# Cross-attention scores and values of a transformer kernel: fp32 matmuls exchanged for three fp32r passes over split operands

## Chip, cores and metric

The kernel runs on one core of one Trainium2 chip. The metric is the device time of one launch in microseconds. TensorE (PE in the rows) does the matmuls, VectorE (DVE) and ScalarE (ACT) the work between them, SyncE (SP) issues most of the DMAs.

## What is computed

The program is two transformer blocks in a row on a 512 x 1024 input. The second block contains, twice (layers 0 and 1), a cross-attention from 512 positions into 256 memory tokens with 4 heads of 256 features:

```
q = rmsnorm_2((h @ w_q).reshape(B, S, X_HEADS, X_HEAD_DIM), q_gain)
kv = (mem_n @ w_kv).reshape(B, M, 2, X_HEADS, X_HEAD_DIM)
k = rmsnorm_2(kv[:, :, 0], k_gain)
v = kv[:, :, 1]
s = jnp.einsum('bqhd,bkhd->bhqk', q, k).astype(jnp.float32) * (X_HEAD_DIM ** -0.5)
p = jax.nn.softmax(s, axis=-1)
o = jnp.einsum('bhqk,bkhd->bqhd', p.astype(v.dtype), v)
return o.reshape(B, S, D_MODEL) @ w_o
```

Around it stand the feed-forward networks, a sliding-window attention with gated linear attention, a differential attention and a stick-breaking attention. They are not touched by the change.

## The kernel before

Every large product is made as three fp32r matmuls over operands split in two: a high part (the value rounded to fp32r) and a low part (the value less its high part). The product is then high*high + high*low + low*high. Lines 606 to 608 are the three passes of a weight slab, lines 1134 to 1138 and 1156 to 1158 those of the memory's keys and values. The weights come as slabs of 128 x 2048 through two landing buffers `w_raw`; ScalarE rounds each to `w_hi` (`high`, line 1351) and VectorE subtracts to `w_lo` (`low`, line 2049). Each of the two holds four slabs.

The products of the cross-attention itself are different: the scores (line 1196) and the values (line 1235) are plain fp32 matmuls of 128 x 256, which the trace records as two matmul records each.

Cross-attention, function `cross` on each engine, runs in two parts. First come projections: keys and values of head 0, then the queries of the four heads, with the norms on ScalarE and VectorE behind them. Then TensorE runs a loop over eight items (four heads, two halves of 256 positions each) plus two steps in which the pipeline empties. Step `i` of this loop is, on TensorE:

1. scores of item `i` (4 matmuls),
2. in steps 1, 3 and 4 the sums of squares of a key head (`sum_squares`, line 639),
3. a projection that lies beside the items: keys of heads 1, 2, 3 in steps 0, 2, 3, values of head 1 in step 1, and a half of the values of heads 2 and 3 in each of the steps 4 to 7; in step 8, four tiles of the output projection instead,
4. the four transposes (line 1220) of the probabilities of item `i-1`,
5. the values of item `i-2` (4 matmuls); in step 9 two tiles of the output projection go ahead of them.

VectorE works through its own loop in the order in which it is written, and the order is fixed by hand. Step `i` is: in steps 4, 6, 8 and 10 first the four instructions (`operand`, lines 1904 and 1906) that cut the outputs of one head for the output projection; then the row maxima of item `i` (lines 2725 and 2728), the scaling of item `i-1`'s probabilities (`probabilities`, lines 2182 to 2188), the norms of a query or key head (`norm_queries`, `norm_keys`, line 1916), the copy of the projected keys or values out of PSUM (`keep_keys` line 2652, `keep_values` line 2659), and `low` for a weight slab. In step 8 the probabilities of item 7 go ahead of the operands.

ScalarE makes the exponentials (line 1824), the inverse norms (lines 1387, 1389), `high`, the copy `copy_turned` of the transposed probabilities from PSUM to `cr_pt` (line 1539) and the squares of the keys.

Both layers run the same code. VectorE instructions are mostly followed by a wait for the engine's own semaphore (`done`), so that they do not overlap.

Of the kernel before, what the change touches and what calls it, by code (L numbers as in the profile page):

```python
# [15 lines left out]
P = 128  # L16
SEQ = 512
# [135 lines left out]
def build(nc, wstream, gains, conv_w, lam_in, base, rope, later, gla_masks, alibi, gate_up,  # L153
          x_in, p_in, mem_in, out):
    ctx = ExitStack()
    with ctx:
# [41 lines left out]
        with ExitStack() as s:  # L198
            cr_q = sb("cr_q", [P, KT, SEQ], FP32, s)
# [6 lines left out]
            cr_pt = sb("cr_pt", [P, 2, 4 * P], FP32, s)  # L206
# [22 lines left out]
        with ExitStack() as s:  # L229
            od_hi_even = sb("od_hi_even", [P, 2, FAR], FP32R, s)  # L230
        sums = sb("sums", [P, SEQ])
# [51 lines left out]
        with ExitStack() as s:  # L283
            cr_pad = sb("cr_pad", [P, 8], FP32, s)
            cr_mhi = sb("cr_mhi", [P, KT, MEM], FP32R, s)
            cr_mlo = sb("cr_mlo", [P, KT, MEM], FP32R, s)
            cr_v = sb("cr_v", [P, 2, D], FP32, s)
        with ExitStack() as s:
# [52 lines left out]
        pt_copied = sem("pt_copied")  # L341
        pv_ready = sem("pv_ready")
# [118 lines left out]
        def key_parts():  # L461

            return query_hi[:, 1, 0:MEM], query_lo[:, 1, 0:MEM]

# [116 lines left out]
        def _(pe):  # L581
# [533 lines left out]
            def cross(at, layer):  # L1115
# [70 lines left out]
                for i in range(N + 2):  # L1186
                    if i < N:
                        h, half = CROSS_ITEMS[i]
                        if half == 0:
                            pe.wait_ge(rs_used, job0 + (5 + h if h else 2))  # L1190
                        if i >= 2:
                            pe.wait_ge(e_ready, i0 + i - 1)
                        for j in range(2):
                            at_q = slice((2 * half + j) * P, (2 * half + j + 1) * P)
                            for k in range(2):
                                mm = mm_(ps[:, 4 + i % 2, j * MEM:(j + 1) * MEM], cr_q[:, 2 * h + k, at_q],
                                         cr_k[:, 2 * h + k, :], start=(k == 0), stop=(k == 1))
# [13 lines left out]
                    if 1 <= i <= N:  # L1211
# [3 lines left out]
                        if i >= 3:  # L1215
                            pe.wait_ge(pt_copied, i0 + i - 2)
# [6 lines left out]
                    if i >= 2:  # L1223
                        h, half = CROSS_ITEMS[i - 2]
                        pe.wait_ge(pt_copied, i0 + i - 1)
                        pe.wait_ge(acc_free, at + VALUE_SLABS[h] + 3)
# [6 lines left out]
                        for d in range(2):  # L1233
                            for a in range(2):
                                mm = mm_(ps[:, out_bank(h, d), half * 256:half * 256 + 256],  # L1235
                                         cr_v[:, a, (2 * h + d) * P:(2 * h + d + 1) * P],
                                         cr_pt[:, (i - 2) % 2, a * 256:a * 256 + 256], start=(a == 0), stop=(a == 1))
# [657 lines left out]
        def _(dve):  # L1895
# [752 lines left out]
            def cross(of, at, layer):  # L2648
# [30 lines left out]

                def first_keys():  # L2680
# [17 lines left out]
                for h in range(4):  # L2698
# [5 lines left out]
                    add_pair(h)  # L2704
                    low(at + QUERY_SLABS[h] + 4)
                i0, N = n["it"], len(CROSS_ITEMS)
                for i in range(N + 3):
                    it = i0 + i
                    if i >= 3 and CROSS_ITEMS[i - 3][1]:
                        h = CROSS_ITEMS[i - 3][0]  # L2710
                        if i == N:
                            probabilities(it - 1, cr_s, MEM, ring=2)
                        for d in range(2):
# [258 lines left out]
```

## Time and profile before

| what | value |
|---|---|
| time, median of 3 runs (lowest to highest) | 2560.86 us (2560.44 to 2560.95) |
| the profiled execution's own time | 2560.95 us |
| its span, from first to last instruction | 2559.1 us |
| TensorE busy | 2540.1 us, 99% of the span |
| VectorE busy | 1596.4 us, 62% |
| ScalarE busy | 911.6 us, 36% |
| granted TensorE clock over the span | 1.000 |
| the eight-item loop of layer 0 | 1278.58 to 1352.5 us |

A TensorE record lasts longer than the time by which it holds up the next one, since matmuls are pipelined; what a matmul costs is read from start to start.

### The profile page before, as it was taken

The page shows a single profiled execution, that of the slowest core. Times are in us where ns is not written, and L with a number is a line of the kernel's source. Part 1 is how long each engine was busy: PE and PEld are TensorE (multiplying, and loading weights), DVE is VectorE, ACT ScalarE, POOL GpSimd, SP SyncE. Part 2 cuts the span into 40 slices and gives each one's busy share as a digit, 9 for nine tenths or more (in the row PEclk, how much of TensorE's full clock was granted, in tenths as well). Part 3 has the DMA queues.
Part 4 walks back from the last instruction along what each step waited for, and adds up shares of the span by engine and source line. Part 5 has one row for each costly group of instructions (what it writes and reads, how often), then busy time and mean ns, then how long its engine had stood idle before and what let it go on. Part 6 is the DMA issues. An engine that isn't in the chain of part 4 may idle for free.

```text
span 2559.1 us, 31974 instructions
## 1 busy us (share of the span) xinstructions
PE 2540.1 (99%) x12548; PEld 2106.0 (82%) x12548; DVE 1596.4 (62%) x1976; ACT 911.6 (36%) x1184; POOL 10.2 (0%) x24
## 2 busy tenths in 40 slices
PE   9999999999999999999999999999999999999999
PEld 7888888778888888877898888888886888888887
DVE  6444468866444468677765747476357665775755
ACT  5222234543222245344443323233146343432322
POOL 0000001000000000000000000000000000000000
PEclk9999999999999999999999999999999999999999
DMA  5323233112322232212321222323210232232322
GB/s 184 101 83 100 96 110 121 67 50 99 103 87 98 99 115 101 99 50 99 132 97 63 104 101 83 114 83 124 94 66 13 87 116 83 84 116 83 100 97 82
DMA packets 37410, 241.91 MB, mean 95 GB/s; under 512 B 4416, under 2 KB 7280, under 8 KB 9136
## 3 DMA queue, kind: packets, MB, share of 16 engines
q1 hardware_dynamic: 34736, 233.78, 26.9%
q10 hardware_dynamic: 1920, 5.22, 0.6%
q0 software_dynamic: 640, 1.31, 0.2%
q8 instruction: 81, 1.33, 0.2%
q14 instruction: 33, 0.27, 0.0%
HBM read 236.89 MB, written 2.10 MB: 93 GB/s over the span
## 4 chain that ended last, share of the span: by engine, by line
PE 93%; DVE 5%; ACT 1%; issue 1%; DMA 0%; DVEq 0%; ACTq 0%
PE ps L606 24%; PE ps L607 24%; PE ps L608 24%; PE ps L1235 1%; PE ps L624 1%; PE ps L626 1%; PE ps L625 1%; PE ps L767 1%; PE ps L1268 1%; PE ps L1292 1%; PE ps L1283 1%; DVE w_lo L2049 1%; PE ps L769 1%; PE ps L768 1%; PE ps L1304 1%
## 5 line engine op out<-in xcount | busy, mean ns | idle before, releaser
L606 PE MATMUL ps<-op_hi,w_hi 128*128 128x512 f32 x2056 | 800.9, 390 | 0.2 <-DVE op_lo L1930 0.2
L607 PE MATMUL ps<-op_lo,w_hi 128*128 128x512 f32 x2056 | 800.5, 389 | 0.0
L608 PE MATMUL ps<-op_hi,w_lo 128*128 128x512 f32 x2056 | 800.4, 389 | 0.0
L1351 ACT ACTIVATE w_hi<-w_raw 128x2048 fp32r<-128x2048 f32 x217 | 414.2, 1910 | 485.9 <-PE ps L608 299.8
L2049 DVE TENSOR_TENSOR w_lo<-w_raw,w_hi 128x2048 fp32r<-128x2048 f32 x217 | 497.0, 2292 | 38.9 <-ACT w_hi L1351 22.5
L606 PEld LDWEIGHTS ps<-op_hi,w_hi 128*128 128x128 f32 x2056 | 386.4, 188 | 81.5 <-issue 1.4
L608 PEld LDWEIGHTS ps<-op_hi,w_lo 128*128 128x128 f32 x2056 | 386.3, 188 | 80.5
L607 PEld LDWEIGHTS ps<-op_lo,w_hi 128*128 128x128 f32 x2056 | 386.3, 188 | 80.0
L2014 DVE SCALAR_TENSOR_TENSOR x<-ps,x 128x512 f32<-128x512 f32 x134 | 92.6, 691 | 310.8 <-PE ps L608 293.1
L606 PE MATMUL ps<-h_hi,w_hi 128*128 128x512 f32 x692 | 269.5, 389 | 0.0
L608 PE MATMUL ps<-h_hi,w_lo 128*128 128x512 f32 x692 | 269.2, 389 | 0.0
L607 PE MATMUL ps<-h_lo,w_hi 128*128 128x512 f32 x692 | 269.2, 389 | 0.0
L2097 DVE TENSOR_TENSOR sil<-ps,rs_x 128x512 f32<-128x512 f32 x44 | 30.4, 691 | 211.8 <-PE ps L608 209.4
L1464 ACT ACTIVATE conv_buf<-u_buf,cw 128x512 f32<-128x512 f32 x88 | 63.2, 725 | 261.0 <-DVE u_buf L2080 261.0
L606 PEld LDWEIGHTS ps<-h_hi,w_hi 128*128 128x128 f32 x692 | 129.9, 188 | 27.5 <-DVE h_lo L2108 0.6
L608 PEld LDWEIGHTS ps<-h_hi,w_lo 128*128 128x128 f32 x692 | 129.9, 188 | 27.0
L607 PEld LDWEIGHTS ps<-h_lo,w_hi 128*128 128x128 f32 x692 | 129.9, 188 | 27.0
L1469 ACT ACTIVATE sil<-sil 128x512 f32<-128x512 f32 x44 | 27.8, 632 | 338.3 <-DVE sil L2097 338.3
L2080 DVE TENSOR_TENSOR u_buf<-ps,rs_x 128x512 f32<-128x512 f32 x44 | 30.4, 691 | 82.2 <-PE ps L608 82.2
L2089 DVE SCALAR_TENSOR_TENSOR conv_buf<-u_buf,cw,conv_buf 128x511 f32<-128x511 f32 x88 | 66.1, 751 | 20.5 <-ACT conv_buf L1464 11.0
L1396 ACT ACTIVATE sq<-x 128x512 f32<-128x512 f32 x80 | 48.2, 621 | 77.9 <-DVE sums L1942 74.2
L2092 DVE SCALAR_TENSOR_TENSOR conv_buf<-u_buf,cw,conv_buf 128x510 f32<-128x510 f32 x88 | 66.0, 750 | 10.5 <-DVE conv_buf L2089 1.4
(373 smaller groups left out, 3083.2 us busy)
## 6 DMA issues: line engine op xcount, KB each, us to landing
w_raw<-in_wstream_dram SPq DMA_DIRECT2D x217, 1024.0 KB, 4.8
cr_m<-in_mem_dram ACTq DMA_DIRECT2D x2, 1024.0 KB, 4.9
w_raw<-in_wstream_dram SPq DMA_DIRECT2D x7, 256.0 KB, 7.7
x<-in_x_dram SPq DMA_DIRECT2D x3, 512.0 KB, 7.5
out_dram<-x SPq DMA_DIRECT2D x3, 512.0 KB, 2.6
m_s<-m_q POOLq DMA_DIRECT2D x16, 64.0 KB, 2.5
ev_s<-in_alibi_dram ACTq DMA_DIRECT2D x1, 1024.0 KB, 5.0
m_c<-in_rope_dram ACTq DMA_DIRECT2D x1, 640.0 KB, 4.2
```

What stands on the lines that cost most here:

```text
L606: mm_(o, w_hi[:, c % 4, w], hi[:, k, 0:cols], start=(k == 0), stop=False)
L607: mm_(o, w_hi[:, c % 4, w], lo[:, k, 0:cols], start=False, stop=False)
L608: mm = mm_(o, w_lo[:, c % 4, w], hi[:, k, 0:cols], start=False, stop=(k == kt - 1))
L1351: f_(w_hi[:, c % 4, :], w_raw[:, c % 2, :], ACT.Copy).then_inc(w_hi_ready, 1)
L1396: f_(to[:, n["xsq"] % 2, 0:src.shape[1]], src, ACT.Square).then_inc(xsq_ready, 1)
L1464: f_(conv_buf[:, j, :], u_buf[:, j, :], ACT.Copy, scale=tap).then_inc(tap_ready, 1)
L2014: ins = v.scalar_tensor_tensor(x[:, 2 * d + j, :], acc(c, j), half, x[:, 2 * d + j, :], ALU.mult, ALU.add)
L2049: v.tensor_tensor(w_lo[:, c % 4, :], w_raw[:, c % 2, :], w_hi[:, c % 4, :].bitcast(FP32), ALU.subtract).then_inc(w_ready, 1)
L2080: v.tensor_tensor(u_buf[:, 0, :], acc(c, 0), rs_x[:], ALU.mult).then_inc(scaled_ready, 1)
L2089: v.scalar_tensor_tensor(buf[:, 1:SEQ], u[:, 0:SEQ - 1], w1, buf[:, 1:SEQ], ALU.mult, ALU.add).then_inc(v_step, 1)
L2092: v.scalar_tensor_tensor(buf[:, 2:SEQ], u[:, 0:SEQ - 2], w0, buf[:, 2:SEQ], ALU.mult, ALU.add).then_inc(v_step if j else conv_ready, 1)
L2097: v.tensor_tensor(sil[:, c % 2, :], acc(c, 0), rs_x[:], ALU.mult).then_inc(scaled_ready, 1)
```

## The change

The scores and values of the cross-attention become three fp32r passes each, like the projections. The operands have to be split for this, all of it on VectorE: `cut_queries`, `cut_keys` and `cut_values` are a rounding copy and a subtraction per head, and `cut_turned` is one subtraction per item. The high part of the turned probabilities is what ScalarE writes to `cr_pt` anyway, which now has the type fp32r. The values of an item are multiplied in two groups: eight matmuls with the high part of the probabilities, then a wait for `pt_cut`, then four with the low part. The low parts of queries, keys and values take the place of the originals in memory; the high parts lie in the operand buffers `op_hi` and `op_lo`, those of head 0's queries and keys in a new tile `cr_first`. Scores wait for `score_parts`, values for `value_parts`. Tile allocations and semaphores are left out here.

```diff
                         h, half = CROSS_ITEMS[i]
                         if half == 0:
-                            pe.wait_ge(rs_used, job0 + (5 + h if h else 2))
+                            pe.wait_ge(score_parts, 4 * layer + h + 1)
...
                             for k in range(2):
-                                mm = mm_(ps[:, 4 + i % 2, j * MEM:(j + 1) * MEM], cr_q[:, 2 * h + k, at_q],
-                                         cr_k[:, 2 * h + k, :], start=(k == 0), stop=(k == 1))
+                                o, q_hi, k_hi = ps[:, 4 + i % 2, j * MEM:(j + 1) * MEM], queries_hi(h), keys_hi(h)
+                                mm_(o, q_hi[:, k, at_q], k_hi[:, k, :], start=(k == 0), stop=False)
+                                mm_(o, q_hi[:, k, at_q], cr_klo[:, 2 * h + k, :], start=False, stop=False)
+                                mm = mm_(o, cr_qlo[:, 2 * h + k, at_q], k_hi[:, k, :], start=False, stop=(k == 1))
...
                         if i >= 3:
-                            pe.wait_ge(pt_copied, i0 + i - 2)
+                            pe.wait_ge(pt_cut, N * layer + i - 2)
...
-                        pe.wait_ge(acc_free, at + VALUE_SLABS[h] + 3)
+                        pe.wait_ge(value_parts, 4 * layer + h + 1)
...
                         for d in range(2):
                             for a in range(2):
-                                mm = mm_(ps[:, out_bank(h, d), half * 256:half * 256 + 256],
-                                         cr_v[:, a, (2 * h + d) * P:(2 * h + d + 1) * P],
-                                         cr_pt[:, (i - 2) % 2, a * 256:a * 256 + 256], start=(a == 0), stop=(a == 1))
+                                o, at_h = ps[:, out_bank(h, d), half * 256:half * 256 + 256], slice(d * P, (d + 1) * P)
+                                p_hi = cr_pt[:, (i - 2) % 2, a * 256:a * 256 + 256]
+                                mm_(o, values_hi(h)[:, a, at_h], p_hi, start=(a == 0), stop=False)
+                                mm_(o, cr_vlo[:, a, (2 * h + d) * P:(2 * h + d + 1) * P], p_hi, start=False, stop=False)
+                        pe.wait_ge(pt_cut, N * layer + i - 1)
+                        for d in range(2):
+                            for a in range(2):
+                                o, at_h = ps[:, out_bank(h, d), half * 256:half * 256 + 256], slice(d * P, (d + 1) * P)
+                                p_lo = cr_ptlo[:, (i - 2) % 2, a * 256:a * 256 + 256]
+                                mm = mm_(o, values_hi(h)[:, a, at_h], p_lo, start=False, stop=(a == 1))
...
+                def cut_queries(h):
+                    heads = slice(2 * h, 2 * h + 2)
+                    v.tensor_copy(queries_hi(h), cr_q[:, heads, :]).then_inc(v_step, 1)
+                    done(v_step)
+                    last = v_step if h else score_parts
+                    v.tensor_tensor(cr_qlo[:, heads, :], cr_q[:, heads, :], queries_hi(h).bitcast(FP32),
+                                    ALU.subtract).then_inc(last, 1)
+                    done(last)
...
+                def cut_turned(it):
+                    dve.wait_ge(pt_copied, it + 1)
+                    v.tensor_tensor(cr_ptlo[:, it % 2, :], ps[:, 6 + it % 2, :], cr_pt[:, it % 2, :].bitcast(FP32),
+                                    ALU.subtract).then_inc(pt_cut, 1)
+                    done(pt_cut)
...
                     add_pair(h)
+                    if h == 0:
+                        cut_keys(0)
+                    elif h == 1:
+                        cut_queries(0)
                     low(at + QUERY_SLABS[h] + 4)
...
                         if i == N:
                             probabilities(it - 1, cr_s, MEM, ring=2)
+                            cut_turned(it - 2)
...
                     if 1 <= i < N:
                         probabilities(it - 1, cr_s, MEM, ring=2)
+                    if 2 <= i < N or i == N + 1:
+                        cut_turned(it - 2)
                     if i == 1:
                         norm_queries(3)
                     if i < N:
                         if i in CROSS_SUMS:
                             norm_keys(CROSS_SUMS[i][0])
+                            cut_keys(CROSS_SUMS[i][0])
...
                     if i - 1 in CROSS_ENDS:
                         low(at + CROSS_ENDS[i - 1] + 4)
+                    if i in (0, 2, 3):
+                        cut_queries(max(i, 1))
+                    if i in (1, 2, 5, 7):
+                        cut_values(i // 2 if i > 2 else i - 1)
```

## Rows read from the trace of the kernel before

**Rows 1.** The page: busy time of the engines.

```profile
PE 2540.1 (99%) x12548; PEld 2106.0 (82%) x12548; DVE 1596.4 (62%) x1976; ACT 911.6 (36%) x1184; POOL 10.2 (0%) x24
```

**Rows 2.** Busy time by stretch: stretch, length, then each engine's busy time (instructions).

```profile
1278.58:1352.30 73.72, 72.66 (x482) 66.93 (x480) 50.18 (x79) 33.09 (x65) 0.00 (x0) 1.00 0.28 92
```

**Rows 3.** TensorE's timeline in steps 0 to 3 of layer 0: start, length, what.

```profile
1280.43 0.28 PE L1136 MATMUL ps<-cr_mlo,w_hi 128*128 128x256 f32 x1
...
1285.96 1.02 PE L683 MATMUL ps<-sq,sums_r 128*128 128x512 f32 x2
...
1288.92 1.10 PE L639 MATMUL ps<-sq,sums_r 128*128 128x256 f32 x4 [0.21 <-ACT sq L1363]
...
1289.98 0.28 PE L1157 MATMUL ps<-w_hi,cr_mlo 128*128 128x256 f32 x1
...
1295.32 0.60 PE L1220 MATMUL ps<-ident,cr_s 128*128 128x128 f32 x4
...
1303.37 1.89 PE L1235 MATMUL ps<-cr_pt,cr_v 128*128 128x256 f32 x8
1305.10 1.89 PE L1196 MATMUL ps<-cr_k,cr_q 128*128 128x256 f32 x8
```

**Rows 4.** VectorE's instructions over the whole span, grouped by line and form.

```profile
L2771 DVE TENSOR_TENSOR od_lo<-od_s,od_hi 128x1024 fp32r<-128x1024 f32 x8 | 9.8, 1225 | 0.3
...
L2769 DVE CAST od_hi<-od_s 128x1024 fp32r<-128x1024 f32 x8 | 5.5, 694 | 0.3
...
L1960 DVE TENSOR_TENSOR query_lo<-sq,query_hi 128x512 fp32r<-128x512 f32 x6 | 4.2, 693 | 0.2
...
L1958 DVE CAST even_hi<-sq 128x512 fp32r<-128x512 f32 x8 | 3.4, 428 | 0.3
```

**Rows 5.** VectorE's timeline in the loop of layer 0; the bracket is idle time before.

```profile
1288.82 0.69 DVE L2725 TENSOR_REDUCE stat<-ps 128x2 f32<-128x512 f32 x1 [1.89 <-PE ps L1196]
...
1289.75 0.17 DVE L2182 RECIPROCAL stat<-stat 128x2 f32<-128x2 f32 x1
...
1290.73 1.54 DVE L1916 SCALAR_TENSOR_TENSOR cr_q<-cr_q,g_sb,rs 128x512 f32<-128x512 f32 x2
...
1295.59 0.69 DVE L2659 TENSOR_TENSOR cr_v<-ps,rs_col 128x512 f32<-128x512 f32 x1 [2.29 <-PE ps L1158]
...
1298.53 0.68 DVE L2725 TENSOR_REDUCE stat<-ps 128x2 f32<-128x512 f32 x1
...
1307.03 0.69 DVE L2725 TENSOR_REDUCE stat<-ps 128x2 f32<-128x512 f32 x1 [0.81 <-PE ps L1196]
...
1309.89 1.01 DVE L1916 SCALAR_TENSOR_TENSOR cr_k<-cr_k,g_sb,rs 128x256 f32<-128x256 f32 x2 [1.00 <-ACT rs L1389]
...
1316.55 0.68 DVE L1904 CAST op_hi<-ps 128x512 fp32r<-128x512 f32 x1
...
1319.44 0.69 DVE L2725 TENSOR_REDUCE stat<-ps 128x2 f32<-128x512 f32 x1
```

**Rows 6.** VectorE's timeline, step 6 of the same loop.

```profile
1333.64 0.69 DVE L2725 TENSOR_REDUCE stat<-ps 128x2 f32<-128x512 f32 x1
...
1337.49 2.29 DVE L2049 TENSOR_TENSOR w_lo<-w_raw,w_hi 128x2048 fp32r<-128x2048 f32 x1 [1.98 <-ACT w_hi L1351]
```

**Rows 7.** TensorE's timeline, steps 4 and 9 of the same loop.

```profile
1321.37 0.66 PE L1220 MATMUL ps<-ident,cr_s 128*128 128x128 f32 x4 [0.37 <-DVE cr_s L2188]
...
1350.74 1.89 PE L1235 MATMUL ps<-cr_pt,cr_v 128*128 128x256 f32 x8
```

**Rows 8.** TensorE's timeline at the start of the kernel, same columns.

```profile
6.25 2.50 PE L841 MATMUL ps<-w_hi 128*128 128x256 f32 x10 [6.25 <-ACT w_hi L1571]
...
10.68 0.63 PE L608 MATMUL ps<-op_hi,w_lo 128*128 128x512 f32 x1
...
20.73 0.39 PE L606 MATMUL ps<-op_hi,w_hi 128*128 128x512 f32 x1
20.96 0.39 PE L607 MATMUL ps<-op_lo,w_hi 128*128 128x512 f32 x1
```

More of the change, by code:

```diff
@@ L198, in build @@
         with ExitStack() as s:
+            with ExitStack() as t:
+                cr_qlo = sb("cr_qlo", [P, KT, SEQ], FP32R, t)
             cr_q = sb("cr_q", [P, KT, SEQ], FP32, s)
@@ L205, in build @@
             cr_s = sb("cr_s", [P, 2, 2, MEM], FP32, s)
-            cr_pt = sb("cr_pt", [P, 2, 4 * P], FP32, s)
+            cr_pt = sb("cr_pt", [P, 2, 4 * P], FP32R, s)
+            with ExitStack() as t:
+                cr_klo = sb("cr_klo", [P, KT, MEM], FP32R, t)
             cr_k = sb("cr_k", [P, KT, MEM], FP32, s)
@@ L230, in build @@
             od_hi_even = sb("od_hi_even", [P, 2, FAR], FP32R, s)
+        with ExitStack() as s:
+            cr_ptlo = sb("cr_ptlo", [P, 2, 4 * P], FP32R, s)
         sums = sb("sums", [P, SEQ])
@@ L286, in build @@
             cr_mlo = sb("cr_mlo", [P, KT, MEM], FP32R, s)
+            with ExitStack() as t:
+                cr_vlo = sb("cr_vlo", [P, 2, D], FP32R, t)
             cr_v = sb("cr_v", [P, 2, D], FP32, s)
+            cr_first = sb("cr_first", [P, 3, SEQ], FP32R, s)
         with ExitStack() as s:
@@ L341, in build @@
         pt_copied = sem("pt_copied")
+        score_parts = sem("score_parts")
+        value_parts = sem("value_parts")
+        pt_cut = sem("pt_cut")
         pv_ready = sem("pv_ready")
@@ L463, in key_parts, with queries_hi, keys_hi, values_hi @@
             return query_hi[:, 1, 0:MEM], query_lo[:, 1, 0:MEM]
+        def queries_hi(h):
+            return op_hi[:, 2 * h:2 * h + 2, :] if h else cr_first[:, 0:2, :]
+        def keys_hi(h):
+            tile = op_lo[:, 2 * h, :] if h else cr_first[:, 2, :]
+            return tile.rearrange("p (k n) -> p k n", k=2)
+        def values_hi(h):
+            return op_lo[:, 2 * h + 1, :].rearrange("p (a n) -> p a n", a=2)
         def query_parts(h):
@@ L2678, in norm_queries, with cut_keys, cut_values @@
                     head_norm([cr_q[:, 2 * h + k, :] for k in range(2)], [gcol(f"xq{layer}", k) for k in range(2)])
+                def cut_queries(h):
[6 more added lines that the diff above has]
+                    done(last)
+                def cut_keys(h):
+                    heads = slice(2 * h, 2 * h + 2)
+                    v.tensor_copy(keys_hi(h), cr_k[:, heads, :]).then_inc(v_step, 1)
+                    done(v_step)
+                    last = score_parts if h else v_step
+                    v.tensor_tensor(cr_klo[:, heads, :], cr_k[:, heads, :], keys_hi(h).bitcast(FP32),
+                                    ALU.subtract).then_inc(last, 1)
+                    done(last)
+                def cut_values(h):
+                    head = slice(h * 256, (h + 1) * 256)
+                    v.tensor_copy(values_hi(h), cr_v[:, :, head]).then_inc(v_step, 1)
+                    done(v_step)
+                    v.tensor_tensor(cr_vlo[:, :, head], cr_v[:, :, head], values_hi(h).bitcast(FP32),
+                                    ALU.subtract).then_inc(value_parts, 1)
+                    done(value_parts)
+                def cut_turned(it):
[3 more added lines that the diff above has]
+                    done(pt_cut)
                 def first_keys():
```

## The prediction

> **What bounds the kernel.** I read the page first: TensorE is busy for 99% of the span, VectorE for 62% [rows 1]. That says only that, averaged over the kernel, time taken from TensorE is time gained. The change lies in two short loops, one a layer, so the second view is the busy time of that stretch: of 73.72 us TensorE is busy for 72.66 and VectorE for 50.18 [rows 2]. VectorE's 79 instructions each stand about 0.03 us apart, 2.4 us, so it has some 21.1 us free. The third view is TensorE's timeline there, for what a matmul costs from start to start; the fourth VectorE's timeline, since the change puts work into a queue in a fixed order, and the brackets show where that queue had slack. Layer 1 has the same waits, so I work out layer 0 and double it.
>
> **What TensorE saves.** The eight fp32 records of an item's values hold it from 1303.37 to 1305.10, 1.73 us; the scores have the same number and form of records [rows 3]. Each becomes twelve fp32r matmuls of 128 x 256, a form that the projections already have: from 1280.43 to 1285.96 there are 47 of them, 0.118 us each, from 1289.98 to 1295.32 again 47, 0.114 each [rows 3]. Twelve cost 1.36 to 1.41, so a group saves 0.32 to 0.37. There are 16 groups a layer: 5.1 to 5.9 us a layer, 10 to 12 us in all, if nothing else decides.
>
> **What VectorE gets.** All forms of the new instructions are in the trace: a rounding copy of 128x512 takes 0.43, of 128x1024 0.69; a subtraction 0.69 and 1.225 [rows 4]. With 0.03 behind each, a cut of a key or value head is 1.19 us, of a query head 1.98, a `cut_turned` 0.73 (one source is in PSUM; the operands' line 1906 has that form and the four of a head go by at 0.72 each, 1316.55 to 1319.44 [rows 5]). In the loop: three query heads 5.9, three key heads 3.6, four value heads 4.7, eight turned items 5.8, together 20.0 us. The cuts of keys 0 and queries 0 come earlier, while TensorE projects queries, where VectorE has waits of 1.5 and 3.7 us behind them; they cost nothing, and 0 to 0.4 us if that cover is thinner than I read. So VectorE needs 50.2 + 2.4 + 20.0 = 72.6 us for a loop that TensorE alone would now do in about 68. VectorE becomes the bound. Whether the loop gets longer than 73.7 depends on where its queue still has to wait, so I walk through it.
>
> **The walk, layer 0.** Units from [rows 5]: maxima and probabilities 1.91 (1288.82 to 1290.73), the probabilities alone 0.98 (from 1289.75); norms of queries 1.57, of keys 1.04; a `keep` with a `low` 2.94 (1295.59 to 1298.53), so `low` 2.21 and `keep` 0.73; operands of a head 2.89.
> Step 0: VectorE was free at 1286.93. `cut_queries(1)` fills this gap; maxima(1) start at 1288.92, 0.1 late. TensorE gains 0.7 by now and loses it: it waits at line 639 for ScalarE's squares until 1288.92 [rows 3], and ScalarE is not faster.
> Step 1: 1.91 + 1.57 + 1.04 + `cut_keys(1)` ends at 1294.6; the wait for the projected values until 1295.59 covers that. `low` ends at 1298.53 as before, then `cut_values(0)`: maxima(2) 1299.7.
> Step 2: +1.91 + 0.73 = 1302.35; the key projection ends at 1302.6, and with 0.27 of latency `keep_keys(2)` goes at 1302.85; `low` to 1305.8, `cut_queries(2)` and `cut_values(1)` to 1308.95. Maxima(3) were at 1307.03.
> Step 3: maxima, probabilities and `cut_turned(1)` to 1311.6; `norm_keys(2)` needs ScalarE's inverse norm, 2.86 after the maxima (1307.03 to 1309.89 before): 1311.8; then 1.04 + 1.19 + 0.73 + 2.21 + 1.98 (`cut_queries(3)`) = 1318.95.
> Step 4: operands to 1321.85, maxima and probabilities to 1323.75. TensorE, which had been up to 1.4 us ahead of before, is ready for the transposes of item 3 at about 1319.1: it stands idle for 4.7 us. They start at 1323.8; before, 1321.37 [rows 7]. `cut_turned(2)`, the wait for ScalarE again (1324.7), `norm_keys(3)`, `cut_keys(3)`, `low`: 1329.1.
> Step 5: 1.91 + 0.73 + 0.73 + `cut_values(2)` = 1333.7.
> Step 6: operands to 1336.55, +1.91 + 0.73 = 1339.2. `low` waits for ScalarE's `high`, 3.85 after the maxima (1333.64 to 1337.49 [rows 6]): 1340.4 to 1342.6. This is the only real gap left in VectorE's queue, 1.2 us.
> Step 7: 1.91 + 0.73 + 0.73 + 1.19 = 1347.2. Step 8: 0.98 + 0.73 + 2.89 + 2.21 = 1354.0. Step 9: `cut_turned(7)`, queued behind that `low` though TensorE needs it first, to 1354.7.
> TensorE: the transposes of item 6 go at 1344.6, and with output tiles, item 7's transposes and item 6's values it is through the eight high matmuls of item 7 at 1353.4. It waits for `pt_cut`, restarts 0.1 late, and four matmuls (0.46) end at 1355.25. Before they ended at 1350.74 + 1.73 = 1352.47 [rows 7]. Behind this everything is paced by TensorE as before (the last operands are ready 1.2 us before it wants them), so the loss stays: 2.8 us a layer, 5.6 in all.
> The other new waits cost nothing: `score_parts` for head 2 is set at 1314.05, just when TensorE arrives (up to 0.1, and covered by the idle time in step 4); `value_parts` and the other `pt_cut` are set earlier than wanted. `low` comes up to 4.5 us later for six slabs, and so do SyncE's loads into the freed buffer, but each slab's `high` follows more than 5 us behind its load, and DMA engines are 28% busy [rows 2]. ScalarE's copy into fp32r costs what its copy into fp32 did: bound 0 to 0.1 us an item, in its idle time.
>
> **A rule that speaks against it further.** The trace shows what idleness can do: behind the 6.25 us of idle time at the start ten 128x256 matmuls took 2.50 us, 0.23 apart, twice the 0.114 above, which is the 1.2 instead of the 2.4 GHz level, and a 512-column record still lasts 0.63 at 10.68 against 0.39 at 20.73 [rows 3, 8]. The granted clock is 1.00 in the whole of the loop [rows 2], where the longest idle stretch was 0.5 us; mine has one of 4.7. If the clock fell there for the 4.6 us that it was low at the start, the transposes of item 3 and the values and scores behind them would take 2.3 us more; part of that VectorE hides, and by the walk the scores of item 5 and the values of item 3 would each come about 0.5 late for VectorE, 0.6 us a layer together.
> The Trainium skill ("TensorE: Matmul & The Clock Gate", section "Why this matters for your kernels") has it that idle gaps between bursts of matmuls put the clock back to half; by it the time would be some 1.2 us longer. The trace agrees for the start, and shows no such gap later.
>
> **Rivals.** *VectorE keeps up* (faster, 0.07): the additions fit into the 21.1 us of free time, and TensorE paces the loop. For it: 20.0 is less than 21.1. Against: in the walk 3.1 us of it stay unused (1.0 in step 1, 0.5 in step 2, 0.2 and 0.2 for the inverse norms, 1.2 in step 6), and `cut_queries(2)`, `cut_values(1)` and `cut_queries(3)`, 5.15 us, all stand ahead of step 4's transposes. The point is the transposes of item 3: VectorE would have to be through probabilities(3) at 1319.1 instead of 1323.75. It would give 2560.95 - 11.8 + 1.4 (step 1's wait) = 2550.5 us.
> *The queue loses less* (within 0.2%, 0.36): my walk keeps three waits for ScalarE, 0.2 + 0.2 + 1.2 us. If they close, the loop is 1.1 us longer instead of 2.8: 2563.2 us. For it: ScalarE is busy for 33 of 73.7 us. Against: its work hangs on VectorE's maxima, at distances that the rows show. A walk that is 10% too long lies here too.
> *The clock falls as well* (0.15): 2560.95 + 5.6 + 1.2 = 2567.8 us.
> *Plain forecast* (0.42): 2560.95 + 5.6 = 2566.5 us.
>
> **The numbers.** The sum is made against the profiled execution, 2560.95 us, 0.09 above the median of the three runs. 0.2%, about what a measurement of this kernel can tell from no change, is 5.1 us, so a forecast of 5.6 lies close to the line. Slower by more: 0.57 (forecast and clock); within: 0.36; faster: 0.07. The likeliest case's own range is 2565.4 to 2568, from 2.3 to 3.5 us a layer: TensorE's pace of 0.114 or 0.118, restarts behind waits, cover thinner ahead of the loop. The range for 8 in 10 leaves out the fast rival and some of each tail: 2559.5 to 2571, its upper end by the clock case with the 10 new idle stretches of two layers each costing 0.3 us more at their restarts.
>
> **What the new profile would show.** Right: VectorE nearly without a gap from 1298 to 1354, about 70 us busy in the loop, one gap of over 1 us before the `low` of step 6; TensorE idle for 4 to 5 us before the transposes of item 3 and 1.3 to 1.5 us each before those of items 4 and 5 and before the low matmuls of item 7; twelve matmuls in 1.36 to 1.41 us; a loop of 76 to 77 us, twice. Wrong: a loop below 74 us, or no wait of TensorE for `cr_s` in step 4. What would make me wrong: VectorE's copies slower or faster on these layouts than in [rows 4], ScalarE earlier than its distances, or a clock below 1.00 behind step 4.

## The result, and the profile of the changed kernel

The changed kernel takes 2568.28 us (median of 8 runs, 2567.45 to 2570.03); the kernel before, run beside it, 2561.46 us (2560.44 to 2564.51). The ratio is 1.0025, 95% interval 1.0016 to 1.0035: slower by 6.8 us. The profiled execution took 2568.33 us, its span is 2566.5 us, and the granted clock over the span is 0.998.

The page's line of busy times: against [rows 1], TensorE is busy for 4.8 us less, and VectorE for 44.1 us more.

```profile
PE 2535.3 (99%) x12676; PEld 2107.6 (82%) x12676; DVE 1640.5 (64%) x2040; ACT 911.9 (36%) x1184; POOL 10.2 (0%) x24
```

The two loops, by stretch: length, busy time of TensorE, of its weight loads, of VectorE, ScalarE and GpSimd, granted clock, DMA share, GB/s.

```profile
1278.81:1355.86 77.05, 70.21 (x545) 67.69 (x544) 68.58 (x106) 33.12 (x65) 0.00 (x0) 0.98 0.26 85
2086.29:2164.05 77.76, 70.95 (x545) 68.44 (x544) 68.69 (x106) 33.13 (x65) 0.00 (x0) 0.96 0.26 85
```

The loop of layer 0 begins with the first scores at 1278.81 and ends where the output projection goes on, at 1355.86: 77.05 us, against 1278.58 to 1352.47, 73.9, before. Layer 1 takes 77.76. VectorE's busy time went from 50.2 to 68.6 us, and the clock is no longer 1.00 as in [rows 2].

TensorE's timeline, layer 0: start, length, line, what, and in brackets how long it had stood idle and for whom.

```profile
1278.81 0.28 PE L1222 MATMUL ps<-cr_first 128*128 128x256 f32 x1
1278.92 0.28 PE L1223 MATMUL ps<-cr_klo,cr_first 128*128 128x256 f32 x1
1279.04 0.28 PE L1224 MATMUL ps<-cr_first,cr_qlo 128*128 128x256 f32 x1
...
1289.16 0.67 PE L664 MATMUL ps<-sq,sums_r 128*128 128x256 f32 x2 [0.82 <-ACT sq L1397]
...
1304.95 0.28 PE L1222 MATMUL ps<-op_lo,op_hi 128*128 128x256 f32 x1
...
1306.39 0.60 PE L664 MATMUL ps<-sq,sums_r 128*128 128x256 f32 x2
...
1324.31 0.79 PE L1247 MATMUL ps<-ident,cr_s 128*128 128x128 f32 x4 [4.24 <-DVE cr_s L2222]
1324.75 0.56 PE L1264 MATMUL ps<-cr_pt,op_lo 128*128 128x256 f32 x1
1325.33 0.41 PE L1264 MATMUL ps<-cr_pt,op_lo 128*128 128x256 f32 x1
...
1355.28 0.74 PE L1271 MATMUL ps<-cr_ptlo,op_lo 128*128 128x256 f32 x4 [1.02 <-DVE cr_ptlo L2742]
1355.86 0.40 PE L1193 MATMUL ps<-op_hi,w_hi 128*128 128x512 f32 x1
```

What to see: twelve score matmuls take 1.44 us (1304.95 to 1306.39) where the eight records before took 1.73 [rows 3]. The transposes of item 3 (line 1247), which waited 0.37 us before [rows 7], wait 4.24. The last low pass waits 1.02 for the cut of the turned probabilities. The lead that TensorE gained in step 0 is gone in step 1, where it waits 0.82 for ScalarE's squares.

VectorE's timeline of the same loop, same columns, answers to [rows 5] and [rows 6].

```profile
1287.17 0.69 DVE L2716 CAST op_hi<-cr_q 128x1024 fp32r<-128x1024 f32 x1
1287.90 1.23 DVE L2719 TENSOR_TENSOR cr_qlo<-cr_q,op_hi 128x1024 fp32r<-128x1024 f32 x1
...
1299.95 0.69 DVE L2796 TENSOR_REDUCE stat<-ps 128x2 f32<-128x512 f32 x1
...
1303.37 0.69 DVE L2686 TENSOR_TENSOR cr_k<-ps,rs_mem 128x512 f32<-128x512 f32 x1 [0.82 <-PE ps L1163]
...
1309.47 0.69 DVE L2796 TENSOR_REDUCE stat<-ps 128x2 f32<-128x512 f32 x1
...
1319.48 0.69 DVE L1938 CAST op_hi<-ps 128x512 fp32r<-128x512 f32 x1
...
1322.38 0.69 DVE L2796 TENSOR_REDUCE stat<-ps 128x2 f32<-128x512 f32 x1
...
1323.90 0.35 DVE L2222 TENSOR_SCALAR cr_s<-cr_s,stat 128x256 f32<-128x256 f32 x1
...
1340.98 2.29 DVE L2083 TENSOR_TENSOR w_lo<-w_raw,w_hi 128x2048 fp32r<-128x2048 f32 x1 [1.26 <-ACT w_hi L1385]
```

Between 1299.95 and 1355 VectorE has only the bracketed waits of 0.82 and 1.26 us and two of 0.27 left. The operands of step 4 start at 1319.48, 2.93 later than at 1316.55 in [rows 5].

The granted clock behind the long wait, two microseconds at a time, columns as for the loops:

```profile
1320.00:1324.00 4.00, 0.07 (x1) 0.00 (x0) 3.73 (x9) 0.69 (x3) 0.00 (x0) 1.00 0.49 205
1324.00:1326.00 2.00, 1.69 (x10) 1.69 (x11) 1.66 (x4) 1.97 (x5) 0.00 (x0) 0.68 0.00 0
1326.00:1328.00 2.00, 2.00 (x11) 2.00 (x11) 1.90 (x4) 1.43 (x2) 0.00 (x0) 0.50 0.00 0
1328.00:1330.00 2.00, 2.00 (x18) 2.00 (x18) 2.00 (x2) 0.00 (x0) 0.00 (x0) 0.97 0.00 0
```

TensorE does nothing for 4 us, and then works for some 3.4 us at 0.50, the 1.2 GHz level: 11 matmuls in 2 us, where two microseconds later there are 18. In layer 1 the clock is low for 6.8 us, from 1.5 us before the end of the same wait.

### The profile page after: what moved, and what is told of

The parts are those of the page before. It is cut to its first block, busy times and chain, and to the rows that moved or that the text cites. A ratio compares the mean times of both kernels' runs of the same rounds, so it can differ in the third digit from the quotient of the medians.

```text
span 2566.5 us, 32312 instructions
## 1 busy us (share of the span) xinstructions
PE 2535.3 (99%) x12676; PEld 2107.6 (82%) x12676; DVE 1640.5 (64%) x2040; ACT 911.9 (36%) x1184; POOL 10.2 (0%) x24
## 4 chain that ended last, share of the span: by engine, by line
PE 90%; DVE 7%; ACT 2%; issue 1%; DMA 0%; POOL 0%; DVEq 0%; ACTq 0%
PE ps L631 24%; PE ps L633 24%; PE ps L632 24%; DVE w_lo L2083 1%; PE ps L649 1%; PE ps L651 1%; PE ps L650 1%; PE ps L792 1%; PE ps L1302 1%; PE ps L1326 1%; PE ps L1317 1%; PE ps L794 1%; PE ps L793 1%; PE ps L1338 1%; PE ps L842 1%
## 5 line engine op out<-in xcount | busy, mean ns | idle before, releaser
L1430 ACT ACTIVATE sq<-x 128x512 f32<-128x512 f32 x80 | 48.2, 622 | 77.2 <-DVE sums L1976 73.4
```

The lines of the kernel that those rows point to most:

```text
L1430: f_(to[:, n["xsq"] % 2, 0:src.shape[1]], src, ACT.Square).then_inc(xsq_ready, 1)
```

## The experiments

All times are medians, with the ratio to the kernel before in runs of the same group on the same chip. The kernel before had 2561.22 us beside the first four experiments of the table, 2561.46 beside the next four, 2561.74 beside the next three and 2561.59 beside the last. Each experiment has 11 runs, the first on GpSimd 6. The changed kernel has its 8 runs from another group, so a difference between two groups can be off by some 0.5 us, by which their kernels before differ. "Waits" are TensorE's idle times ahead of the transposes of items 3, 4 and 5 in layer 0, VectorE's busy time is that from 1278 to 1360 us. "Loops" are the lengths in layer 0 and layer 1, from the first scores to the end of the last values, in the one profiled execution.

| kernel | us | ratio (95%) | waits 3 / 4 / 5 | VectorE | loops |
|---|---|---|---|---|---|
| before | | | 0.37 / 0 / 0.47 | 53.1 | 73.9 / 74.1 |
| changed | 2568.28 | 1.0025 (1.0016 to 1.0035) | 4.24 / 0 / 0.76 | 71.6 | 77.05 / 77.76 |
| no cuts in the loop | 2556.9 | 0.9982 (0.9973 to 0.9991) | 0.86 / 0.53 / 0.67 | 54.8 | 71.73 / 71.72 |
| scores alone | 2566.8 | 1.0019 (1.001 to 1.0028) | 2.57 / 0 / 0.69 | 61.2 | 76.7 / 76.7 |
| values alone | 2560.15 | 0.9994 (0.9985 to 1.0004) | 0.67 / 0.24 / 0.81 | 63.1 | 74.02 / 74.02 |
| TensorE kept busy in the wait | 2567.74 | 1.0024 (1.0015 to 1.0033) | 0.52 / 0.95 / 1.10 | 71.6 | 77.23 / 77.22 |
| last turned cut earlier | 2567.57 | 1.0024 (1.0015 to 1.0033) | 4.24 / 0 / 0.75 | 71.2 | 75.94 / 76.60 |
| three cuts moved | 2566.21 | 1.0015 (1.0006 to 1.0024) | 2.50 / 2.71 / 0.29 | 71.6 | 76.69 / 75.74 |
| six cuts on GpSimd | 2569.32 | 1.0033 (1.002 to 1.0045) | 0.88 / 0.95 / 0.67 | 71.0 | 77.66 / 77.72 |
| the same, last turned cut earlier | 2566.78 | 1.0019 (1.0009 to 1.0028) | 0.88 / 0.95 / 0.67 | 71.1 | 76.39 / 77.95 |
| values alone, last turned cut earlier | 2559.7 | 0.999 (0.998 to 0.9999) | 0.67 / 0.24 / 0.80 | 63.8 | 72.95 / 72.76 |
| the same, rounding on ScalarE | 2559.87 | 0.999 (0.9981 to 0.9999) | 0.67 / 0.24 / 1.10 | 62.0 | 73.25 / 73.06 |
| all, rounding on ScalarE | 2561.47 | 0.9998 (0.9989 to 1.0007) | 2.57 / 0 / 1.40 | 67.8 | 74.73 / 74.41 |
| the same, two cuts moved | 2562.16 | 1.0003 (0.9994 to 1.0012) | 1.14 / 1.98 / 1.40 | 68.3 | 74.14 / 75.28 |

### Is it VectorE's added work?

**No cuts in the loop.** TensorE's twelve matmuls stay, VectorE's cuts in the loop go; where a wait needs it, a write of one column stands for a cut. The kernel leaves out the low parts and multiplies what lies in the high buffers in their place.

```diff
-                                mm_(o, q_hi[:, k, at_q], cr_klo[:, 2 * h + k, :], start=False, stop=False)
+                                mm_(o, q_hi[:, k, at_q], k_hi[:, k, :], start=False, stop=False)
...
                 def cut_values(h):
+                    thin(value_parts)
+                    return
...
```

> Every cut in the loop is reduced to one write of one column that sets the semaphore, and the matmuls read high parts where they would read low ones, so TensorE's instructions and waits are those of the changed kernel and only VectorE's 20 us a layer are left out (the output lacks the low parts). My theory, that VectorE's queue is what lengthens the loop: no wait of 4 us in step 4, a loop of 68 to 70 us instead of 77.1, about 2551 us (10 us below the kernel before). Rival, that three passes save little or that the split of the values with its second wait costs: the loop stays above 73 us, 2558 us or more.

It took 2556.9 us, some 11 less than the changed kernel. VectorE's cuts are the cause of the loss: without them the same number of matmuls makes the kernel faster, not slower. The size was missed: 2551 us and loops of 68 to 70 had been expected, and the loops take 71.7. So it gained only 4.3 us on the kernel before, not the 10 to 12 that TensorE's records promise. TensorE then waits 1.04 us for ScalarE's squares in step 1 and 0.86, 0.53 and 0.67 us for probabilities, 3.1 us a layer; without them the loop would take 68.6. In the kernel before it waited 0.21 us for the squares [rows 3], and 0.37 [rows 7] and 0.47 us (the table) for probabilities: ScalarE and VectorE, with no work added, were already that close to setting the pace.

**Scores alone and values alone.** One product in three passes with its cuts, the other plain fp32 as before. From the edit of the second:

```diff
-                                mm_(o, q_hi[:, k, at_q], k_hi[:, k, :], start=(k == 0), stop=False)
-                                mm_(o, q_hi[:, k, at_q], cr_klo[:, 2 * h + k, :], start=False, stop=False)
-                                mm = mm_(o, cr_qlo[:, 2 * h + k, at_q], k_hi[:, k, :], start=False, stop=(k == 1))
+                                mm = mm_(ps[:, 4 + i % 2, j * MEM:(j + 1) * MEM], cr_q[:, 2 * h + k, at_q],
+                                         cr_k[:, 2 * h + k, :], start=(k == 0), stop=(k == 1))
...
```

> Only the scores are three passes; values stay fp32, without cut_values and cut_turned. VectorE gets 9.5 us more a layer in the loop. The walk through its queue: transposes of item 3 at 1.2 us later than before, of item 4 1.7 us later, a part given back at the end because TensorE is the later one there: 1.0 to 1.2 us longer a layer, about 2563.7 us (2 to 2.5 above the kernel before). Rival, loss in proportion to VectorE's added work (9.5 of 20 us): 3.3 us above. Rival, that TensorE's saving counts in full: 5 us below.

> Only the values are three passes; scores stay fp32, without cut_queries and cut_keys. VectorE gets 10.5 us more a layer, more than with scores only. The walk: these pieces fall into gaps of the queue, transposes of item 3 at the same time as before, and the loop ends within 0.3 us of before: 2561 to 2562 us, no change. Rival, loss in proportion to the added work (10.5 of 20 us): 3.6 us above the kernel before.

They are not alike. Values alone are at 2560.15 us, not to be told from the kernel before (1.1 us below it), though they give VectorE slightly more busy time in the same 82 us than the scores do (63.1 against 61.2). Scores alone are at 2566.8, 5.6 above it. The walk had the values right; for the scores it said 2563.7 and was 3.1 too low. TensorE's line in the scores' kernel:

```profile
1322.27 0.66 PE L1247 MATMUL ps<-ident,cr_s 128*128 128x128 f32 x4 [2.57 <-DVE cr_s L2215]
```

The cuts of queries 1 to 3 and of keys 1 and 2, 8.3 us by the prediction's prices, all lie ahead of this row; of the values' work only the cuts of values 0 and 1 and two turned cuts do, 3.8 us, and the rest is spread to step 9. So it is not the whole amount on VectorE that decides, but what stands ahead of the probabilities of item 3.

### Is it the clock?

Sixteen matmuls whose result nobody reads were put into TensorE's wait in step 4.

```diff
+                    if i == 4:
+                        pe.wait_ge(pt_cut, N * layer + 2)
+                        for _ in range(16):
+                            mm_(ps[:, 7, :], ones_r, cr_mhi[:, 0:2, :], start=True, stop=True)
```

> The changed kernel with 16 matmuls of 128x512 (3.6 us) put into TensorE's wait in step 4, into the PSUM bank that the transposes overwrite: nothing else moves. The granted clock should not fall behind the wait. By my walk the fall cost 0 in layer 0 (where it lasted 3.4 us) and 0.7 in layer 1 (6.8 us): 0.7 us below the changed kernel, 2567.6. Rival, the fall of the clock is the main part of the loss: 2562 us or less.

TensorE's row of item 3's transposes in this kernel, and the windows behind it:

```profile
1324.94 0.44 PE L1251 MATMUL ps<-ident,cr_s 128*128 128x128 f32 x2 [0.52 <-DVE cr_s L2226]
```

```profile
1324.00:1326.00 2.00, 1.49 (x11) 1.06 (x10) 1.63 (x5) 1.97 (x7) 0.00 (x0) 1.00 0.00 0
1326.00:1328.00 2.00, 2.00 (x19) 2.00 (x18) 1.90 (x4) 2.00 (x2) 0.00 (x0) 1.00 0.00 0
```

The clock stays at 1.00 in both loops and the time falls by 0.5 us, to 2567.74, which the two intervals would not tell from nothing. The wait is still there, only filled. The loops say the same: 77.23 and 77.22 us, where the changed kernel has 77.05 and 77.76, so the fall cost nothing in layer 0 and 0.5 us in layer 1. The clock is a small part of the loss. Six of the eleven runs have a mean clock of 1.000, with a median of 2567.3, the other five, at 0.999, one of 2569.2. The profiled one, of the second kind, has a fall elsewhere, told below.

### Is it the order on VectorE?

**Last turned cut earlier.** The low part of the slab in step 9 goes behind `cut_turned` of item 7.

```diff
-                    if i - 1 in CROSS_ENDS:
-                        low(at + CROSS_ENDS[i - 1] + 4)
+                    if i - 1 in CROSS_ENDS and i < N or i == N + 1:
+                        low(at + CROSS_ENDS[min(i, N) - 1] + 4)
```

> Only the order of two pieces on VectorE in the last step changes: the low part of the projection block of step 9 goes behind the cut of the last turned probabilities. In the changed kernel TensorE stood 1.02 us at the last values' low pass, for that cut. If VectorE's order at the loop's end carries part of the loss, each layer is about 1.0 us shorter: 2566.3 us. If the end of the loop is set by the amount of VectorE's work alone, whatever its order, nothing changes: 2568.3 us.

**Three cuts moved.** This too, and the cut of queries 3 to step 4, that of values 0 to step 2, each behind the turned cut. The lines that take them out of their old places are left out here.

```diff
                     if 2 <= i < N or i == N + 1:
                         cut_turned(it - 2)
+                    if i == 2:
+                        cut_values(0)
+                    if i == 4:
+                        cut_queries(3)
+                    if i == N + 1:
+                        low(at + CROSS_ENDS[N - 1] + 4)
...
```

> The same work as in the changed kernel; on VectorE the cut of queries 3 goes from step 3 to step 4, behind the turned cut, the cut of values 0 behind the turned cut of step 2, and the low part of step 9 behind the last turned cut. By the walk the 4.2 us wait in step 4 shrinks by the 1.92 us of the query cut, the clock doesn't fall behind it, and the 1.0 us at the end goes: about 2.9 us a layer, 2562.5 us. If VectorE's total is the bound, the wait only moves to steps 5 to 7 and only the 1.0 us of the end is won: 2566.3 us.

The first is 0.7 us under the changed kernel, within what the two intervals leave open. Its loops (stretches, columns as above) show more:

```profile
1277.80:1353.74 75.94, 70.13 (x546) 67.82 (x545) 67.91 (x106) 33.11 (x65) 0.00 (x0) 0.98 0.25 86
2085.33:2161.93 76.60, 70.81 (x545) 68.50 (x544) 67.99 (x106) 33.12 (x65) 0.00 (x0) 0.96 0.25 85
```

The 1.02 us wait is gone from both, and they are 1.1 and 1.2 us shorter than the changed kernel's, as the theory of the order had it. But in this trace the clock falls once more than in the changed kernel's, at 1894 us, far behind the loop; all eleven runs have a mean clock of 0.997 or 0.996, where six of the changed kernel's eight have 0.998. Such a fall costs some 2 us (last section), which is what the loops gained. That it hid the gain in all eleven runs is the likely reading, not a shown one. The second came to 2566.21, close to what the bound on the total says. Its transposes of items 3, 4 and 5:

```profile
1322.21 0.66 PE L1247 MATMUL ps<-ident,cr_s 128*128 128x128 f32 x4 [2.50 <-DVE cr_s L2222]
...
1331.26 0.66 PE L1247 MATMUL ps<-ident,cr_s 128*128 128x128 f32 x4 [2.71 <-DVE cr_s L2222]
...
1339.39 0.66 PE L1247 MATMUL ps<-ident,cr_s 128*128 128x128 f32 x4 [0.29 <-DVE cr_s L2222]
```

1.74 us of the first wait are gone, and 2.71 stand one step later, where there was none; in layer 1 the three waits are 2.26, 1.21 and 1.10. The two loops together take 152.4 us, as against 152.5 with the last turned cut alone moved. VectorE has no gap in which the moved cut could hide, so moving it only moves the wait.

### Can another engine take the cuts?

**Six cuts on GpSimd**, which does nothing in this loop: queries 1 to 3 and values 0 to 2, each a copy and a subtraction as on VectorE.

```diff
+                def pool_cut(hi, lo, src, signal, n):
...
+                    g.tensor_copy(hi, src).then_inc(pool_step, 1)
+                    pool.wait_ge(pool_step, step)
+                    g.tensor_tensor(lo, src, hi.bitcast(FP32), ALU.subtract).then_inc(signal, 1)
...
-                    if i in (0, 2, 3):
-                        cut_queries(max(i, 1))
...
```

> The cuts of queries 1 to 3 and of values 0 to 2 go to GpSimd, which is idle in this loop: 3 x 1.92 + 3 x 1.12 = 9.1 us a layer less on VectorE, which leaves it 63 us. If VectorE's added work is the cause, the loop falls to where the kernel with thin cuts stood or a little below: 2557 us. If GpSimd needs more than about 4 us for a cut and so delivers late, or holds VectorE up in memory, the time stays above 2561 us.

> As the kernel with the cuts on GpSimd, and the low part of step 9 behind the last turned cut as well. If the last turned cut is still what the loop's end waits for, 1.0 us a layer less than it: 2555 us; if VectorE, unloaded, has caught up by then, the same as it, 2557 us.

Both missed: 2569.32 and 2566.78 us, though the second is 2.5 below the first, as if the last turned cut were still what the loop's end waits for. In the one execution that was profiled of each, its loop of layer 0 is 1.3 us shorter; in layer 1, where the clock fell at 2108 us in the second alone, it is 0.2 longer. GpSimd's rows, then VectorE's of the same microseconds:

```profile
1288.15 1.26 POOL L617 TENSOR_TENSOR cr_vlo<-cr_v,op_lo 128x512 fp32r<-128x512 f32 x1
...
1290.59 2.37 POOL L617 TENSOR_TENSOR cr_qlo<-cr_q,op_hi 128x1024 fp32r<-128x1024 f32 x1
...
1296.18 2.45 POOL L617 TENSOR_TENSOR cr_qlo<-cr_q,op_hi 128x1024 fp32r<-128x1024 f32 x1
...
1300.51 2.66 POOL L615 CAST op_lo<-cr_v 128x512 fp32r<-128x512 f32 x1 [1.88 <-DVE cr_v L2733]
```

```profile
1288.18 0.69 DVE L2836 TENSOR_REDUCE stat<-ps 128x2 f32<-128x512 f32 x1
1288.90 0.53 DVE L2839 TENSOR_SCALAR stat<-stat 128x2 f32<-128x2 f32 x1
...
1290.69 2.42 DVE L2262 TENSOR_SCALAR cr_s<-cr_s,stat 128x256 f32<-128x256 f32 x1
...
1296.42 2.50 DVE L2765 CAST op_lo<-cr_k 128x512 fp32r<-128x512 f32 x1
1298.96 0.69 DVE L2768 TENSOR_TENSOR cr_klo<-cr_k,op_lo 128x512 fp32r<-128x512 f32 x1
...
1300.41 2.29 DVE L2123 TENSOR_TENSOR w_lo<-w_raw,w_hi 128x2048 fp32r<-128x2048 f32 x1
```

A scaling that takes 0.35 us in the changed kernel took 2.42, a rounding copy of 0.43 took 2.50, a negation of two columns (0.17) 0.53. Each starts while a GpSimd instruction runs and ends 0 to 0.3 us behind it. It goes the other way too: GpSimd's copy at 1300.51 starts behind a VectorE subtraction (1300.41) and takes 2.66 us, where the same form at 1287.46 took 0.61. The maxima at 1288.18, which read PSUM, took their usual 0.69 beside GpSimd. So 9.1 us of work left VectorE's list, and its busy time fell by 0.6 us. The wait of item 3 did shrink to 0.88 us, but TensorE now waited 2.44 us for the squares in step 1 and 0.91 us for keys 1 (2.34 in layer 1), and the loop ended where it did. The Trainium skill ("SBUF — State Buffer", section "Who interferes with whom") has it that VectorE's two-port instructions and GpSimd share a pair of ports by an exclusive lock, and whoever comes second waits for the whole instruction. The waiting is in this trace, with the rows above; which ports an instruction uses no row here shows.

**Rounding on ScalarE**, three kernels. The first has the values alone in three passes and the last turned cut earlier, with no rounding on ScalarE yet. In the second ScalarE also rounds the high parts of the values, and VectorE keeps the subtraction. The third is the changed kernel with this for the values and for queries 1 to 3, and with the last turned cut earlier. In the second and third the rest of the cut of values 2 also moves to step 6, ahead of the maxima, and that of values 3 to step 8.

```diff
+                def round_queries(h):
+                    act.wait_ge(rs_used, (21, 29)[layer] + (5 if h == 3 else 4))
+                    f_(queries_hi(h), cr_q[:, 2 * h:2 * h + 2, :], ACT.Copy).then_inc(query_high, 1)
...
-                    v.tensor_copy(values_hi(h), cr_v[:, :, head]).then_inc(v_step, 1)
-                    done(v_step)
+                    dve.wait_ge(value_high, 4 * layer + h + 1)
...
+                    if i == 6:
+                        cut_values(2)
...
```

> The kernel with the values alone in three passes (2560.15 us), and the low part of the projection block of step 9 behind the cut of the last turned probabilities. There TensorE waited 0.80 us at the last low pass in each layer. If this wait is real path, the time falls by 1.6 us to 2558.6; in the changed kernel the same move brought only 0.7 of 2.0, so the other theory, that the wait is covered by what comes next, says 2560.

> As the one before it, and the high part of every value is rounded by ScalarE instead of VectorE: 4 x 0.46 us a layer less on VectorE. TensorE waited 0.67, 0.24 and 0.81 us for probabilities in that kernel. If these waits follow VectorE's load, about 1.2 us a layer goes: 2556.2 us, below the kernel before. If they come from the operands that stand ahead of the maxima in any case, nothing goes: 2558.6 us.

> The changed kernel with the high parts of queries 1 to 3 and of all values rounded by ScalarE, and the low part of step 9 behind the last turned cut. Ahead of the probabilities of item 3 VectorE has 3 x 0.73 + 2 x 0.46 = 3.1 us less. If VectorE's work there is the cause of the 4.2 us wait, the wait falls to 1.1 us and the clock stays up: about 4 us a layer less, 2560 us. If ScalarE, whose squares and exponentials TensorE waits for as well, is now late, or hands VectorE its parts late, the time stays above 2564 us.

ScalarE's groups of rounding instructions in the third (line, what, count | busy, mean ns of one | idle before):

```profile
L1845 ACT ACTIVATE op_hi<-cr_q 128x1024 fp32r<-128x1024 f32 x3 | 3.0, 1045 | 0.0
L1841 ACT ACTIVATE op_lo<-cr_v 128x512 fp32r<-128x512 f32 x4 | 2.5, 624 | 0.1
```

The third fell to 2561.47 us, 6.8 below the changed kernel, 1.5 above the 2560 that VectorE's theory gave. Part of this is the last turned cut, which moved as well: with that move alone the loops take 75.94 and 76.60 us, with the rounding on ScalarE too 74.73 and 74.41. So 4 us a layer taken from VectorE's list gave back 1.2 and 2.2 us, and in layer 1 a part of that is the clock, low for 3.41 us instead of 6.83. ScalarE's 5.5 us a layer held up neither of the others: TensorE's wait for the squares stayed at 0.82 us and VectorE's for `high` at 1.26, and VectorE's scalings kept their mean of 0.35 us, where they took 0.43 and 0.61 beside GpSimd. The wait of item 3 went from 4.24 to 2.57, by 1.7 of the 3.1 us taken from ahead of it, and the clock still fell behind it; in the place of the rest VectorE now waits for TensorE's projections, 1.9 and 1.3 us where it waited 1.0 and 0.8. The wait of item 5 grew from 0.76 to 1.40, with the cut of values 2 now ahead of its probabilities. With the values alone the rounding changed nothing for items 3 and 4 (0.67 and 0.24 stayed) and item 5 again waits longer (0.80 and 1.10). That fits the expectation's other reading, that the operands ahead of the maxima set these waits; no run took the operands away. The first and second of these kernels are 0.1% below the kernel before, by intervals that end at 0.9999, and no other kernel here was faster but the one without cuts.

**The same, two cuts moved.** The order of "three cuts moved", on the third kernel.

> The kernel with the rounding on ScalarE (2561.47 us) and, on VectorE, the low part of queries 3 moved from step 3 to step 4 behind the turned cut, and that of values 0 from step 1 to step 2 behind the turned cut. There TensorE still waited 2.57 us for the probabilities of item 3 and 1.40 us for those of item 5. With 4 us a layer less work VectorE should have the room that it lacked when the order alone was changed: the first wait shrinks by the 1.26 us of the moved cut in each layer, 2559.0 us. If the wait only moves to items 4 and 5, as when the order alone was changed, 2561 us or more.

TensorE's transposes of items 3 and 4:

```profile
1320.89 0.55 PE L1249 MATMUL ps<-ident,cr_s 128*128 128x128 f32 x3 [1.14 <-DVE cr_s L2240]
...
1329.22 0.55 PE L1249 MATMUL ps<-ident,cr_s 128*128 128x128 f32 x3 [1.98 <-DVE cr_s L2240]
```

2562.16 us, no better: 1.43 us left the first wait and 1.98 appeared in the second, and the two loops together take 149.4 us against 149.1. VectorE still has no room in step 4, even with 4 us less.

## Why the prediction was right, step by step

Forecast 2566.5 us, range 2559.5 to 2571, slower as the likeliest; measured 2568.28. The sum was made against 2560.95 us, and the kernel before had 2561.46 in the later runs; as a difference, 5.6 was forecast and 6.8 measured. The time lies just above the likeliest case's own range of 2565.4 to 2568 (whose lower end should be 2565.6, by 2.3 us a layer).

- **TensorE's saving**, 0.32 to 0.37 us a group: slightly too high. The scores of item 2 take 1.44 us (1304.95 to 1306.39), a saving of 0.29, since a matmul takes 0.12 here.
- **VectorE's added work**, 20.0 us a layer with gaps: right: the instructions last as in [rows 4] (1.23, 0.69), the 28 of a loop 19.1 us together, 19.9 with 0.03 behind each. The stretch's busy time rose by only 18.4, since the one before had part of the last head's operands in it.
- **VectorE becomes the bound through its order.** Right. Shifted by the 0.23 us by which the loop began later (the loops of the fourteen traces begin anywhere from 1277.5 to 1279.2, so this is no price of the early cuts), the walk had maxima(2) at 1299.9 (1299.95 in the trace), maxima(3) at 1309.2 (1309.47), operands of step 4 at 1319.2 (1319.48), the transposes of item 3 at 1324.0 (1324.31) and the end at 1355.5 (1355.86). The constant 0.3 is one term: I let the key projection of step 2 run at 0.114 us a matmul, and it ran at 0.118, so that `keep_keys(2)` came 0.3 late, and nothing behind it could catch that up.
- **The single wait in step 4**: 4.7 forecast, 4.24 measured. The waits of 1.3 to 1.5 us before items 4 and 5 were 0 and 0.76: TensorE, slowed by the clock and the 0.12, came later to them. With the clock held up they are 0.95 and 1.10. So this part of the forecast profile was wrong, because the plain case had no fall in it.
- **The loss a layer**: 2.8 forecast, 3.15 in layer 0 and 3.65 in layer 1 (74.1 before, 77.76 after). 0.3 of it is the projection's pace, and the 0.5 us that layer 1 lost on top is the longer stretch at the low clock: with the clock held up both loops take 77.2.
- **The clock** is where I gave too little: 0.15 for a fall at the price of 0.6 us a layer. It fell in both layers. The price was too high: 1.2 us had been reckoned for both layers, and holding the clock up was worth 0.4 by the loops and 0.5 by the medians. The time of that rival, 2567.8, is nearer to the result than the forecast's, but partly by luck: its 0.8 us too much for the clock stand in for what the plain walk lacked, 3.3 and 3.1 us a layer at the full clock instead of 2.8.
- **The rival that VectorE keeps up**, 2550.5 us, is refuted twice over: the point named, probabilities(3) in time for 1319.1, was missed by 5 us, and with no cuts in the loop TensorE's saving still isn't had in full (2556.9). The prediction's picture of 21.1 us of free time on VectorE was too kind: 15.7 us of it in layer 0 are waits for TensorE and 5.8 for ScalarE. With three passes and no cuts the waits for TensorE are down to 10.9 us, so they shrink when TensorE gets faster.
- **The rival of the queue that loses less** (three waits for ScalarE close) is out: the 1.26 us in step 6 and the two of 0.27 are in the trace as forecast.

What stays open: scores alone lost 2.8 and 2.6 us in the loops (76.7, where 73.9 and 74.1 stood before), more than my walk's 1.0 to 1.2. Counted from the first scores of layer 0, the transposes of item 3 come 1.8 us later than before (1.2 by the walk) and those of item 4 3.0 later (1.7 by the walk). Between the two lie the 3.41 us for which the clock fell to 0.50, so the fall is likely a part; no run holds the clock up in this kernel.

## What to carry to other kernels

Idle time on the second engine is not room: if it is waiting for the first, it goes as the first gets faster (here from 15.7 to 10.9 us in layer 0's loop, before any work was added). Write out where each new instruction stands in the queue, and what the bounding engine waits for behind it; here some 10 us a layer of cuts for the values cost nothing that can be measured, and 9.5 us a layer for the scores, most of them ahead of one due point, cost 5.6 us in both layers together. Moving work to a later place in a full queue moves the wait, unless nothing behind the new place waits for it, as at the loop's end. Giving work to another engine helps only where the two do not hold each other up: ScalarE took a part of the wait away, GpSimd did not.

## What was unexpected of the hardware

**A fall of the clock behind a short wait.** All fourteen traces have in the stick-breaking attention, between 1889 and 1897 us, a wait of 1.84 or 1.85 us. In seven of them the clock falls to 0.50 for 3.41 us, beginning between 0.3 us before the wait's end and 1.4 us behind it; in the other seven it stays at 1.00. In two kernels that differ in nothing up to there but the end of the first loop, it ends at the same microsecond, and the clock falls in one of them. From 1890 to 1894 us, values alone, then the same with the last turned cut earlier:

```profile
1890.00:1892.00 2.00, 0.55 (x3) 0.56 (x4) 1.93 (x3) 1.45 (x2) 0.00 (x0) 1.00 0.00 0
1892.00:1894.00 2.00, 2.00 (x19) 1.66 (x17) 1.93 (x3) 0.69 (x1) 0.00 (x0) 1.00 0.00 0
```

```profile
1890.00:1892.00 2.00, 0.55 (x2) 0.55 (x3) 1.93 (x3) 1.45 (x2) 0.00 (x0) 0.80 0.00 0
1892.00:1894.00 2.00, 2.00 (x10) 2.00 (x9) 1.93 (x3) 0.00 (x0) 0.00 (x0) 0.50 0.00 0
```

The runs of the second have two levels: three with a mean clock of 1.000 took 2557.79, 2557.80 and 2558.94 us, the eight at 0.999 2559.3 to 2560.89. The expected 2558.6 is what the first three show; one fall costs some 2 us, as in the kernel that kept TensorE busy (medians of 2567.3 against 2569.2) and in the one with the values alone and the rounding on ScalarE (2558.65 against 2560.4). Of all these runs only the profiled ones show where the clock fell. This is as much as what was to be measured, so a gain of 1 to 2 us in one place can be gone for a reason that lies 500 us later. Nor does the length of a wait decide alone: in the kernel with six cuts on GpSimd TensorE stood idle for 2.44 us in step 1 of both layers, and the clock fell behind it in layer 0 and stayed at 1.00 in layer 1; in the kernel with three cuts moved it stayed at 1.00 behind 2.50 us.

**GpSimd beside VectorE** costs VectorE nearly what it takes over (above), and GpSimd itself needs 1.04 us for the copy of 128x1024 at best and 2.37 for the subtraction, 1.5 and 1.9 times VectorE's 0.69 and 1.23.
